# Rows of 272 instead of 264 elements in two activation tables of a float32 decoder trunk

## What is computed

```python
h = _rms_norm(x, norm_g)
z = h @ w_in                        # 2048 x (14*512 + 8 + 4*2048)
...
y_ret, y_gdn, y_sc, y_pool = ...    # four branches of 512 channels
ys = jnp.stack([y_ret, y_gdn, y_sc, y_pool], axis=2)
proj = jnp.einsum('btnc,ncd->btnd', ys, w_branch)
gates = jax.nn.sigmoid(merge_logits.reshape(Bn, T, N_BRANCH, D_MODEL))
merged = jnp.sum(gates * proj, axis=2)
out = x + merged @ w_out
```

## Time and profile before

| | |
|---|---|
| timed runs, us | 2049.89, 2051.46, 2052.07 |
| profiled execution, span of the core's instructions, us | 2049.6 |
| granted TensorE clock, mean share of full | 0.993 |
| TensorE busy | 1992.3 us (97%) |
| weight loads busy | 1976.0 us (96%) |
| VectorE busy | 1346.1 us (66%) |
| ScalarE busy | 1113.6 us (54%) |
| GpSimd busy | 186.5 us (9%) |
| DMA | 348.13 MB, 170 GB/s |

### The profile page before, as it was taken

One profiled execution on the slowest core, in us unless ns is written; L12 is line 12 of the kernel. 1 busy time (PEld: TensorE's weight loads), 2 busy tenths in 40 slices (PEclk: granted clock), 3 DMA queues, 4 the chain that ended last, 5 costly groups with the idle time before them and its releaser, 6 DMA issues.

```text
span 2049.6 us, 50596 instructions
## 1 busy us (share of the span) xinstructions
PE 1992.3 (97%) x16294; PEld 1976.0 (96%) x16294; DVE 1346.1 (66%) x2608; ACT 1113.6 (54%) x2045; POOL 186.5 (9%) x345
## 2 busy tenths in 40 slices
PE   6999999999999999999999999999999999999996
PEld 6999999999999999999999999999999999999996
DVE  7887566755656556666678766676565656566666
ACT  5556556645455555555555655655464645455554
POOL 2111110110101010000011210001010100100000
PEclk9999999999999999999999999999999999999998
DMA  6655555555554545665656555655555555566664
GB/s 209 190 175 172 157 181 162 184 160 156 154 172 135 176 140 167 188 180 180 184 172 184 171 173 155 190 164 175 165 162 160 162 155 149 160 175 179 178 184 161
DMA packets 183252, 348.13 MB, mean 170 GB/s; under 512 B 20592, under 2 KB 20720, under 8 KB 182992
## 3 DMA queue, kind: packets, MB, share of 16 engines
q1 hardware_dynamic: 177552, 326.45, 53.4%
q0 software_dynamic: 5568, 19.80, 3.0%
HBM read 333.61 MB, written 12.56 MB: 169 GB/s over the span
## 4 chain that ended last, share of the span: by engine, by line
PE 90%; DVE 4%; issue 3%; ACT 2%; DMA 1%; DVEq 0%; ACTq 0%; SPq 0%
PE acc L1301 27%; PE acc L1302 27%; PE acc L1303 26%; DMA raw<-w_stream 1%; PE side L1514 1%; PE side L1488 1%; DVE wlo L829 1%; PE side L1512 1%; PE side L1505 1%; ACT whi L540 1%; PE side L1396 1%; PE side L1495 1%; PE side L1402 1%; PE side L1358 1%; DVE act_lo L841 0%
## 5 line engine op out<-in xcount | busy, mean ns | idle before, releaser
L829 DVE TENSOR_TENSOR wlo<-raw,whi 128x512 fp32r<-128x512 f32 x1219 | 828.3, 694 | 488.4 <-ACT whi L540 481.4
L540 ACT ACTIVATE whi<-raw 128x512 fp32r<-128x512 f32 x1219 | 751.5, 628 | 643.7 <-PE acc L1303 553.9
L1301 PE MATMUL acc<-act_hi,whi 128*128 128x264 f32 x3328 | 972.6, 292 | 40.1 <-issue 19.6
L1303 PE MATMUL acc<-act_hi,wlo 128*128 128x264 f32 x3328 | 947.8, 285 | 0.0
L1302 PE MATMUL acc<-act_lo,whi 128*128 128x264 f32 x3328 | 947.2, 285 | 0.0
L1301 PEld LDWEIGHTS acc<-act_hi,whi 128*128 128x128 f32 x3328 | 631.8, 190 | 48.2 <-issue 35.9
L1302 PEld LDWEIGHTS acc<-act_lo,whi 128*128 128x128 f32 x3328 | 632.8, 190 | 0.9
L1303 PEld LDWEIGHTS acc<-act_hi,wlo 128*128 128x128 f32 x3328 | 629.4, 189 | 0.0
L1301 PE MATMUL acc<-y_hi,whi 128*128 128x264 f32 x1536 | 439.9, 286 | 0.0
L1302 PE MATMUL acc<-y_lo,whi 128*128 128x264 f32 x1536 | 435.4, 283 | 0.0
L1303 PE MATMUL acc<-y_hi,wlo 128*128 128x264 f32 x1536 | 434.8, 283 | 0.0
(11 more groups left out here) (267 smaller groups left out, 1438.2 us busy)
## 6 DMA issues: line engine op xcount, KB each, us to landing
raw<-w_stream SPq DMA_DIRECT2D x1220, 256.0 KB, 2.8
state<-ret_in POOLq DMA_DIRECT2D x8, 512.0 KB, 5.5
s_ret<-state POOLq DMA_DIRECT2D x8, 512.0 KB, 4.6
state<-gdn_in POOLq DMA_DIRECT2D x8, 512.0 KB, 5.4
s_gdn<-state POOLq DMA_DIRECT2D x8, 512.0 KB, 6.1
x<-x_in SPq DMA_DIRECT2D x4, 528.0 KB, 6.5
y_out<-wide SPq DMA_DIRECT2D x4, 396.0 KB, 2.8
con<-consts SPq DMA_DIRECT2D x1, 1582.0 KB, 11.8
```

Source lines behind the costliest of these rows:

```text
L540: sc.activation(whi[:, s, :], raw[:, s, :], ACT.Copy).then_inc(hi_ready, 1)
L829: ve.tensor_tensor(wlo[:, s, :], raw[:, s, :], whi[:, s, :].bitcast(F32), ALU.subtract).then_inc(lo_ready, 1)
L1301: mm(acc[bank][:, 0:N], w_h, hi[:, k0 + k, :], start=first and k == 0, stop=False)
L1303: op = mm(acc[bank][:, 0:N], w_l, hi[:, k0 + k, :], start=False, stop=last and k == UK - 1)
```

## The change

The two tables `act_hi` and `act_lo` are allocated with rows of NP = 272 elements, 1088 bytes or 17 times 64, and the program sees the first 264 of each row. `y_hi`, `y_lo`, `x` and `wide` keep rows of 264. Each of the two tables grows by 512 bytes a partition, so `act_lo` moves by 512 bytes and everything allocated behind it by 1024. `act_hi` still begins at a multiple of 64, and now all 16 tiles of both tables do.

```diff
 N = T + NS
+NP = 272
...
         x = sb("x", [KT, N])
-        act_hi = sb("act_hi", [KT, N], F32R)
-        act_lo = sb("act_lo", [KT, N], F32R)
+        act_hi = sb("act_hi", [KT, NP], F32R)[:, :, 0:N]
+        act_lo = sb("act_lo", [KT, NP], F32R)[:, :, 0:N]
```

## The result

The changed kernel takes 2056.86 us in the median against 2052.04 for the kernel before on the same chip. The ratio is 1.0025, with a 95% interval from 1.0018 to 1.0032: slower by a quarter of a per cent, where the prediction had it faster by as much. The time also lies just above the range that was given. One of the 20 executions of the changed kernel took 3244.58 us at a mean granted clock of 0.565 and is left out of the ratio.

What follows compares the result with a forecast made beforehand. TensorE, busy for 97% of the span, was taken to bound the kernel. From 2051.46 us, 5.8 less for 832 units and 0.3 more for registers gave 2045.96, say 2046.0 us; range 2041 to 2056.

Steps and rivals of the forecast that it cites:

- TensorE's stream of matmuls sets the time: Whole kernel: TensorE busy for 97% of the span, weights arriving in time, so time taken from streamed matmuls shortens the end.
- Some 11 ns a matmul lie above its columns: Streamed matmuls at full clock: 120.8 ns against 110 for the columns; only there can a row's start act.
- Even tiles in the trace of before are the changed case: Tiles already at multiples of 64 bytes: four aligned cost 1.44 us, not 1.45; 7 ns a unit taken, 5.8 us less.
- second rival: Units on the changed tables: pace follows place in a 256-byte period, 1.46 us each, 8.3 us more, 2060.1 us; chance 0.15.
- Counts of pieces don't change, so only the phase is left: Rows of 1056 bytes: 17 pieces of 64 touched from either start, so only the phase between matmuls could change.
- Writers at +0.3 us: Fills of the two tables cost nothing more; added register instructions cost 0.2 to 0.6 us, taken as 0.3.
- Moving `act_lo` by 512 bytes: nothing: Address shift of `act_lo` from the longer rows: given no effect on the time either way.
- First rival, no effect: Streamed matmuls: rows at any 32-byte start run alike, fixed cost a matmul; 2051.8 us; chance 0.30.
- Third rival, the large gain: Streamed matmuls: without half-line starts supply keeps up, 110 ns each, 108 us less, 1943.7 us; chance 0.03.
- The test named ahead: Changed kernel's timeline: a turn of stage G should last 23.09 us instead of 23.20, and one of stage R keep its time.

Runs made afterwards that it cites:

- the stream alone: Kernels with only the streamed matmuls, everything else in the computation left out: 120.83 ns a matmul in the layout before, 122.78 with rows of 272.

## Why the prediction was wrong, point by point

- *TensorE's stream of matmuls sets the time.* Right. What moved was TensorE's busy time, and the wait of the earlier trace rows grew with it.
- *Some 11 ns a matmul lie above its columns, and a row's start can act only there.* Right in part. The layout moves the pace between 120.0 and 123.3 ns, at most 3.3 of it (with starts 4 bytes off 125.3 in rows of 1056 bytes, 122.2 in rows of 1536). The rest stays at every start: 384 columns take 173.33 ns and 512 take 226.67, both 13.3 above one column for each cycle of 2.4 GHz. The supply of the moving operand is not shown to be its cause.
- *Even tiles in the trace of before are the changed case.* **This is the step that failed.** The differences of the earlier trace rows were real: by exact starts the four even tiles take 1443 ns and the four odd ones 1457. But what a tile costs belongs to a sequence and not to the tile. The new layout keeps the places of the even tiles (128, 192, 0 and 64 in the period) and takes the odd ones from between them, and four such tiles then take 1473 ns in the stream alone, not 1440. The 7 ns less a unit that was taken from that step became 6.2 ns more in the kernel. The prediction had the objection in its last words on the second rival, that the new tiles have no odd neighbour, and didn't put it in the sum.
- *Counts of pieces don't change, so only the phase is left.* The count is right, and it should have led to a wider forecast: a phase can go either way, and the rows bounded it by 8.3 us in size but not in sign. The loss of 5.2 us is inside that.
- *Writers at +0.3 us.* The fills kept their 1.07 us. TensorE's waits for `act_lo` went from 14.6 to 14.9 us; the registers' share is too small to be seen.
- *Moving `act_lo` by 512 bytes: nothing.* Right, ratio 0.9997.
- *First rival, no effect.* Wrong for these tables; it holds for the move of 32 bytes between two slow layouts.
- *Second rival, slower by the place in a 256-byte period.* This is the nearest to what the runs show. It counted the places from the table's start, which itself lies at 128 in the period, so tiles 0 to 3, which it puts at 0 to 96, lie at 128 to 224, and tiles 4 to 7 at 0 to 96. Its price of 10 ns a unit was too high for the kernel's mix and too low for the pure pattern (23 ns), and that its price came near the measured loss is in part luck, for one pattern for all units was wrong: the history picks between several. It had 0.15 and should have had as much as the forecast, for the rows bore on both alike.
- *Third rival, the large gain.* Gone with the second point. The Trainium skill (TensorE: Matmul & The Clock Gate, section "Wait — 56ns, not 53.3ns?") adds 2.5 ns to N / 2.4; the runs show 10 to 13.3 ns here, for float32r with other weights for each matmul, widths from 248 to 512 columns and 32-byte starts.
- *What the Trainium skill says of 16-byte lines* (SBUF — State Buffer, section "Door 1: The DMA port swizzle") gave the first rival its ground. The runs show more than it does: starts at 0, 32 and 64, all at the edge of a line, take 123.3, 121.7 and 120.0 ns. For TensorE's reads the line of 16 bytes is not the only thing that counts.
- *The test named ahead* worked: the turn of G lengthened and that of R kept its time, and from these two the failed step could be read at once. It looked at one layer only; in layer one the turn of G lengthened by 0.37 us and not 0.05.

## What to carry to other kernels

Don't align tiles of a moving operand to 64 bytes because it looks tidy: put the stream alone in a small kernel, walk the start through its 256-byte period, and take a place that stays quick after an interruption (here 64 or 96, all tiles alike, 0.7% less time for each matmul than before and 2.7% less than at 0; only 96 was tried in the kernel). A unit's cost read from a trace holds for the sequence in which it stands, and not for its parts put together anew. And when matmuls are a few nanoseconds apart from what was expected, count time at each granted clock before the gain is read from the end: a few stretches at half clock can take half of it back.

## What the runs showed of the hardware

- With all moving tiles at one place in a period of 256 bytes, float32r matmuls with 264 columns follow each other in 120.0 to 123.3 ns at full clock: quickest at 64 and 96 of the eight 32-byte places (and as quick, 119.99, at 144), slowest at 0 while nothing interrupts them. Weights moved by 32 bytes had no effect (120.83 ns either way).
- At start 0 the pace is 32 columns' time above the columns: 123.33, 126.66 and 133.33 ns at 264, 272 and 288 columns; 173.33 and 226.67 ns at 384 and 512 (these two at start 128). It is not so at 256 columns: 118.67 ns at start 0, and 120.00 at start 128 in rows of 256 elements.
- One layout can run in two repeating patterns (rows of 272: 1473 or 1453.5 ns a unit; start 128: 1440 or 1458.5), by what stood before the stream. In stage G of the changed kernel a pattern lasted for tens of units, the slower in layer one and the quicker in layer two. What in the chip does this isn't shown by any record of the trace, and stays open.
- The room taken from GpSimd's descriptor scratch (8192 bytes instead of 16384) had no cost here: ratio 1.0 (0.9991 to 1.001).
